# Asking for units of gelu and gates sooner in the order of the SyncE DMA queue

## The reference, cut to what matters

```
a   = einsum("td,thkd->thk", xb, u[eb])      # 8 heads, 16 experts each per token
act = gb * gelu(a)                           # gb: softmax of the best scores
y   = einsum("thk,thkd->td", act, v[eb])
```

## Time and profile before

| | us |
|---|---|
| median of 3 runs | 3128.13 |
| the runs | 3126.65, 3128.13, 3140.87 |
| the profiled execution's own time | 3137.47 |
| its span in the trace | 3135.7 |
| TensorE busy | 2998.2 (96%) |
| VectorE busy | 2533.5 (81%) |
| ScalarE busy | 1030.0 (33%) |
| GpSimd busy | 839.7 (27%) |
| mean granted TensorE clock | 0.977 |

### The profile page before, as it was taken

One profiled execution on the slowest core, in us unless ns is written; L12 is line 12 of the kernel. 1 busy time (PEld: TensorE's weight loads), 2 busy tenths in 40 slices (PEclk: granted clock), 3 DMA queues, 4 the chain that ended last, 5 costly groups with the idle time before them and its releaser, 6 DMA issues.

```text
span 3135.7 us, 41987 instructions
## 1 busy us (share of the span) xinstructions
PE 2998.2 (96%) x17373; PEld 2759.4 (88%) x17373; DVE 2533.5 (81%) x3098; ACT 1030.0 (33%) x1081; POOL 839.7 (27%) x380
## 2 busy tenths in 40 slices
PE   5799989989989999999999999989999999999999
PEld 3687765557778899999999999989999999999999
DVE  7986968756673589999988998854989899898985
ACT  4323243341122333333333333323333334333331
POOL 5600000000030013333123333421444444444440
PEclk8999989989999999999999999999999999999999
DMA  9722223347744468888778988987999999999994
GB/s 368 268 94 77 81 85 138 124 168 302 290 159 180 142 228 326 333 333 321 274 266 343 356 346 337 389 330 285 375 395 389 390 392 392 395 386 398 385 399 164
DMA packets 182257, 893.82 MB, mean 285 GB/s; under 512 B 15680, under 2 KB 77248, under 8 KB 85824
## 3 DMA queue, kind: packets, MB, share of 16 engines
q1 hardware_dynamic: 111376, 491.29, 42.4%
q0 software_dynamic: 46080, 335.56, 26.2%
q10 hardware_dynamic: 24624, 64.45, 5.3%
HBM read 836.71 MB, written 54.53 MB: 284 GB/s over the span
## 4 chain that ended last, share of the span: by engine, by line
PE 84%; DVE 10%; DMA 2%; ACT 2%; issue 1%; SPq 0%; ACTq 0%; DVEq 0%; PEldq 0%
PE bank L1909 10%; PE bank L1911 10%; PE bank L1910 10%; PE bank L1968 10%; PE bank L1969 10%; PE bank L1970 10%; PE bank L1606 3%; PE bank L1608 3%; PE bank L1607 3%; DVE ada_w L944 2%; PE bank L1944 2%; PE bank L1843 2%; PE bank L1844 2%; PE bank L1845 2%; DMA ada_w<-wada 1%
## 5 line engine op out<-in xcount | busy, mean ns | idle before, releaser
L475 POOL DMA_INDIRECT u_row<-u_rows,urow_i x128 | 285.6, 2231 | 823.7 <-DVE u_row L1374 559.0
L1909 PE MATMUL bank<-act_hi,w_hi 128*128 128x352 f32 x1376 | 447.7, 325 | 8.0 <-DVE low L906 8.0
L1910 PE MATMUL bank<-act_lo,w_hi 128*128 128x352 f32 x1376 | 445.0, 323 | 0.0
L1968 PE MATMUL bank<-wt_hi,w_hi 128*128 128x352 f32 x1360 | 439.5, 323 | 4.9 <-DVE w_lo L906 4.4
L1969 PE MATMUL bank<-wt_lo,w_hi 128*128 128x352 f32 x1360 | 438.4, 322 | 0.0
L1911 PE MATMUL bank<-act_hi,low 128*128 128x352 f32 x1024 | 332.1, 324 | 0.0
L1911 PE MATMUL bank<-act_hi,w_lo 128*128 128x352 f32 x1024 | 330.3, 323 | 0.0
L1970 PE MATMUL bank<-wt_hi,w_lo 128*128 128x352 f32 x1024 | 330.3, 323 | 0.0
L1970 PE MATMUL bank<-wt_hi,low 128*128 128x352 f32 x1024 | 329.3, 322 | 0.0
L486 POOL DMA_INDIRECT u_row<-v_rows,urow_i x96 | 232.2, 2418 | 271.3 <-DVE y_g L1521 249.5
L1374 DVE SCALAR_TENSOR_TENSOR u_row<-u_row,h2t 128x2048 f32<-128x2048 f32 x128 | 288.9, 2288 | 13.4 <-DMA u_row<-u_rows,urow_i 13.3
(11 more groups left out here) (340 smaller groups left out, 7234.3 us busy)
## 6 DMA issues: line engine op xcount, KB each, us to landing
ada_w<-wada SPq DMA_DIRECT2D x80, 1024.0 KB, 5.5
w_raw<-u SPq DMA_DIRECT2D x64, 1024.0 KB, 5.9
raw<-u SPq DMA_DIRECT2D x64, 1024.0 KB, 5.6
w_raw<-v SPq DMA_DIRECT2D x64, 1024.0 KB, 9.1
raw<-v SPq DMA_DIRECT2D x64, 1024.0 KB, 6.8
w_raw<-win SPq DMA_DIRECT2D x27, 1024.0 KB, 4.9
gelu_scratch<-gelu_s ACTq DMA_DIRECT2D x128, 176.0 KB, 8.4
gate_scratch<-g_chunk ACTq DMA_DIRECT2D x11, 2048.0 KB, 12.2
```

The source lines that it names most:

```text
L475: pool.indirect_dma_start(u_row[n % 3][:], None, urow_d, bass.IndirectOffsetOnAxis(ap=col, axis=0)).then_inc(u_row_loaded[n % 3], 16)
L1909: pe.matmul(out, wh[:, k, :], HD(k), start=(k == 0), stop=False)
L1910: pe.matmul(out, wh[:, k, :], LD(k), start=False, stop=False)
L1968: pe.matmul(o, wh[:, 8 * e + d, :], th, start=begin is not None and e == 0, stop=False)
```

## The change

Line numbers below are those of the file before; in the changed file all lines behind the first hunk are two higher. The arithmetic is the same, no instruction is added or removed, and each wait stays with its instruction.

```
-            for g in range(2, NKEY - 6):
+            for g in range(2, NKEY - 10):
                 load_raw(g)
             for s in range(2):
                 sp.wait_ge(g_stored[s], DMA_LEAD + 16 * ((N_CH + 1 - s) // 2))
                 sp.wait_ge(gelu_stored[s], DMA_LEAD + 16 * 6)
                 sp.wait_ge(hot_used[2 * s + 1], LEAD + N_HOTS // 2)
             load_unit(0)
-            for g in range(NKEY - 6, NKEY - 1):
+            for g in range(NKEY - 10, NKEY - 5):
                 load_raw(g)
             load_unit(1)
+            for g in range(NKEY - 5, NKEY - 1):
+                load_raw(g)
+            load_unit(2)
             for g in range(NKEY - 1, NKEY + 2):
                 load_raw(g)
-            load_unit(2)
             for q in range(2, 128):
                 load_raw(NKEY + q)
                 if q == 2:
                     for s in range(2):
                         sp.wait_ge(gelu_stored[s], DMA_LEAD + 16 * NKEY // 2)
-                if q == 8:
+                if q == 5:
                     load_unit(3)
-                elif q % 4 == 2 and 10 <= q < 122:
-                    load_unit(4 + (q - 10) // 4)
+                elif q % 4 == 0 and 8 <= q < 120:
+                    load_unit(4 + (q - 8) // 4)
```

More of the change, by code:

```diff
@@ L850, in _ @@
                     act.activation(a_g[:], a_g[:], ACT.Gelu_apprx_tanh).then_inc(act_g_ready, 1)
-                if u == 119:
+                if u == 118:
                     weigh_hi(0)
-                if u == 124:
+                if u == 123:
                     weigh_hi(1)
@@ L1500, in _ @@
                     n_dot += 1
-                if n == 119:
+                if n == 120:
                     weigh(0)
@@ L1504, in _ @@
                     weigh_lo(0)
-                elif n == 124:
+                elif n == 125:
                     weigh(1)
```

## The result

| | before | after |
|---|---|---|
| median of 6 runs | 3139.73 us | 3304.96 us |
| the runs | 3126.65 to 3141.86 | 3298.52 to 3307.43 |
| profiled execution | 3137.47 us | 3304.97 us |
| turn of four V jobs, from the issues of units 4 and 31 | 30.55 us | 36.86 us |

The changed kernel takes 1.054 times as long (95% interval 1.0523 to 1.0557, estimated from the single runs; the two medians alone divide to 1.053). The forecast was 3248 us and 3.8%, so the direction was right and the loss came out larger, near the upper end of the range of 3175 to 3325 us. Between the two profiled executions lie 167.5 us. A turn is the stretch from one unit's load to the next, four V jobs. From the issues of units 4 and 31 it is (3184.89 - 2189.55) / 27 after, and (3025.26 - 2200.36) / 27 before.

A forecast was written before the change was run, and what follows sets the result against it. TensorE was taken as the bound (84% of the chain), with VectorE and DMA nearly full. 3137.5 - 25 + 5 + 140 = 3257.5 us, less 9.3 for the profiled execution, gave 3248 us (3.8% more); range 3175 to 3325 us.

The forecast's parts named there:

- the second rival: V stage: the slow clock comes on top in every turn, 76 us more, 3324 us; chance 0.10.
- the V turns: V stage: a turn grows from 30.56 to 35.8 us, 146 us over 28 units, 140 after a credit.
- the passage: From U stage to V stage: asking sooner for units 0 to 2 adds 5 us (0 to 18).
- waits at U jobs 120 and 125 go, less new ones in the passage: U stage: 11.0 and 6.9 us lost to late units go; new delays from units 0 and 2 add 5 us.
- wait at V job 7 goes: V stage: the 7.1 us lost because unit 3 was asked for too late go.
- The unit could not have left sooner, and the wait holds the weights.: V stage: the unit's one buffer frees 15 us after SyncE gets there, holding the weights of two jobs.
- The turn closes on itself through VectorE, SyncE, DMA and ScalarE.: V stage: VectorE idles 5.6 us more each turn and the next unit waits on it; turn 35.8 us.
- unit 4's row: V stage before the change: weights behind unit 4 landed at U + 11.5 us; taken for the held weights.
- VectorE's lead: Start of the V stage: VectorE is 10.5 us ahead, partly used by unit 3; 6 us credited.
- Unit 1 holds the weights of job 123 by some 6 us, within the low part's slack: U stage: unit 1's earlier load delays those weights by some 6 us, with no loss counted.
- The clock rule: V stage: TensorE's slow clock, 2.7 us a turn, fits into the 35.8 us turn and adds nothing.
- The first rival: V stage: VectorE's lead persists, so the hold is a microsecond or two and is swallowed; 3108 us, chance 0.10.

The follow-up runs named there:

- the two buffers: Changed kernel with the gates of units 4 on left out and units taking turns in two buffers; 3124.7 us, ratio 0.9963 to the kernel before.
- the bare wait: Kernel before with unit 3 moved sooner, and SyncE's wait for wtl_ready two loads sooner without the load of units 4 on; ratio 1.0560 to the kernel before.

## Why the prediction was right

The mechanism, the sign and the place of the loss were as forecast. The size was not: 3305 us lie 57 above the forecast of 3248 and only 19 below the 3324 of the second rival, the slow clock on top, so the number alone doesn't choose between the two. The turns do, as shown below. Two terms were off, the V turns in their size and the passage in a step. In us, between the profiled executions:

| term | forecast | measured |
|---|---|---|
| waits at U jobs 120 and 125 go, less new ones in the passage | - 17.9 + 5 | - 0.8 (start of the V stage) |
| wait at V job 7 goes | - 7.1 | - 7 (unit 3 moved alone) |
| the V turns | + 140 | + 175 |
| sum | + 120 | + 167.5 |

The terms explain 47.5 us (167.5 - 120) of the 57. The other 9.3 are what I took off because the profiled execution lay above the median of three runs; with six runs that median is 3139.73 us, above the profiled 3137.47.

The 175 us are the V stage's growth: its first matmul began at 2138.45 before and at 2137.62 after, so 168.2 us of the spans' difference of 167.4 lie in the V stage, and V job 7's 7 us were won within it.

**The unit could not have left sooner, and the wait holds the weights.** Right. Each unit still left when `weigh_lo` ended (2708.90 and 2708.93), and the two buffers and the bare wait showed that the loss is the wait's.

**The turn closes on itself through VectorE, SyncE, DMA and ScalarE.** Right: in 27 turns VectorE's waits for the held weights' high part, 6.7 us each, less the 0.4 us of late gathers of before, make the whole 6.3 us. The turn's length was under-sized, 35.8 us against 36.9. I took the landing of the held weights from unit 4's row, at U + 11.5; ScalarE began on them at U + 12.8 (2721.70) in one turn and U + 11.9 (2757.86) in the next, and over the 27 turns their low parts ended at U + 15.9 to 18.2, 16.7 in the mean, instead of U + 15.6. The rest of the turn, from there to the next U, was as read before, 20.1 us. So 6.3 us a turn, times 27 or 28 turns 170 to 177 us, for the 146 of the sum. The 6 us that I credited for VectorE's lead were hardly there. That the landing came out so near is in part luck: in unit 4's row the weights left 6.6 us behind the unit and took 4.9 us; in the changed kernel those at 2709.78 left 0.9 us behind U and took 11.9 us. I had no reason that the two sums should be alike.

**The passage.** In the V turns only the size was off. Here a step failed: "Unit 1 holds the weights of job 123 by some 6 us, within the low part's slack". SyncE's list in the changed kernel:

```profile
2051.24 0.33 SPq L397 DMA_DIRECT2D raw<-u  x1
2067.70 0.33 SPq L408 DMA_DIRECT2D wt<-gelu_scratch  x1
...
2069.05 0.74 SPq L397 DMA_DIRECT2D raw<-u  x1
2069.84 8.53 SPq L397 DMA_DIRECT2D w_raw<-u  x2
2081.96 0.33 SPq L397 DMA_DIRECT2D raw<-u  x1
2112.57 0.33 SPq L408 DMA_DIRECT2D wt<-gelu_scratch  x1
```

The first row is the weights of U job 122. Those of 123 were due 7.7 us later, at 2058.9, and left at 2069.05, 10 us late. VectorE then stood idle for them:

```profile
2087.31 2.29 DVE L908 TENSOR_TENSOR w_lo<-raw,w_hi 128x2048 fp32r<-128x2048 f32 x1 [15.22 <-ACT w_hi L786]
```

TensorE lost 7.7 us at that place, and 3.4 at U job 127 after unit 2 had stood 30 us in front of its weights. The two old waits went and the same fault made two new ones, one mechanism with the V stage. Instead of 12.9 us won (- 17.9 + 5) the V stage began 0.8 us sooner. I had put the hold at "some 6 us" without working it out and had not written down the slack that should have taken it. Unit 2's term, 2.3 us and the clock, was near. Unit 0, for which I had feared 2 us, cost nothing.

**The clock rule.** Idle time of up to 11.3 us did bring the slow clock, 0.92 on the average of the body for 1.00. It cost nothing beyond the turn, as forecast: VectorE's waits account for all of the turn's growth and leave nothing for TensorE's clock. The second rival needed TensorE on the loop; its waits could be moved from the evictions to the low parts without a gain. The first rival (VectorE runs ahead) and the third (quick landings) are refuted by the turns: in each of the 27 VectorE stood 5.7 us or more for weights.

**What I said the profile would show.** Right: the waits behind `wt_lo`, over 10 us each from unit 4 on; VectorE's idle time in front of the low part, and none in front of `weigh`. Right in kind but too small: turns of 35 to 36 us (36.9), and idle times of 4 to 6 us (6.7). Wrong: that both held tiles would leave within 2 us of the unit, since the second left 3 to 5 us behind it; and that TensorE would wait for low parts over 28 times.

## What to carry to other kernels

Before a load is moved sooner in a queue that issues in order, look up whether its own buffer is free at the new place. If the load already leaves the moment its buffer is free, the new place can only hold what stands behind it. Here a wait of 3.3 us in the turn cost nothing, one of 10.5 us cost 0.7, and one long enough to hold two tiles of weights cost 6.3 us in each turn. And where all resources grow less busy at once, look for a loop of waits: find the engine whose new idle time a turn equals the turn's growth, and don't trust the operand that the busiest engine happens to wait for.

## What was not expected of the hardware

The gates' load, 704 KB in pieces of 512 B, seems to weigh more than its bytes: leaving it out took 2.9 us from a turn (36.86 to 33.98), where 704 KB at the 391 GB/s of the body before are 1.8 us by my estimate. The traces show the pieces: without these loads there are 39873 packets less for 20.2 MB. Whether it is the pieces' size, their meeting the gathers, or something else in the burst wasn't tried apart.
